# Scaling the probabilities instead of the heads' output in a latent attention, with the query transposes moved ahead

## The reference, cut to what matters

```python
q = (c_q @ w_uq).reshape(b, s_len, MLA_HEADS, MLA_NOPE + MLA_ROPE)
q = jnp.concatenate([q[..., :MLA_NOPE], apply_rope(q[..., MLA_NOPE:], positions)], axis=-1)
...
logits = jnp.einsum('bqhd,bkhd->bhqk', qb, kb).astype(jnp.float32) * scale
logits = jnp.where(causal, logits, NEG_INF)
probs = jax.nn.softmax(logits, axis=-1).astype(v.dtype)
outs.append(jnp.einsum('bhqk,bkhd->bqhd', probs, vb))
...
return o.reshape(b, s_len, MLA_HEADS * MLA_V) @ w_o
```

## Time and profile before

| | us |
|---|---|
| median of three runs (1433.08 to 1433.68) | 1433.24 |
| the profiled execution, its own time | 1433.6 |
| its span, first to last instruction | 1431.8 |
| TensorE busy (8258 matmuls) | 1416.1 |
| TensorE's weight loads busy | 1234.8 |
| VectorE busy | 657.7 |
| ScalarE busy | 747.8 |
| GpSimd busy | 1058.2 |

### The profile page before, as it was taken

How to read it: one execution, slowest core, us unless ns; L and a number is a source line. 1 busy time by engine, 2 the same in 40 slices (tenths; PEclk the granted TensorE clock), 3 DMA queues, 4 the chain that set the end, 5 groups by cost and what they waited for, 6 DMA issues and landing times.

```text
span 1431.8 us, 20732 instructions
## 1 busy us (share of the span) xinstructions
PE 1416.1 (99%) x8258; PEld 1234.8 (86%) x8258; DVE 657.7 (46%) x1379; ACT 747.8 (52%) x985; POOL 1058.2 (74%) x262
## 2 busy tenths in 40 slices
PE   9999999999999999999999999999999999999997
PEld 7888888888899899888888889988888899888886
DVE  5546555034333333355440354656650566556614
ACT  7876555354666566665543545435543346354540
POOL 5475988965766656869888677749889577688891
PEclk9999999999999999999999999999999999999999
DMA  7576555546655656455554565255555655365560
GB/s 252 207 270 221 182 201 181 202 164 201 206 172 189 195 178 197 162 192 192 190 188 165 202 245 195 102 206 177 196 214 200 222 187 180 118 232 180 192 220 29
DMA packets 65239, 272.12 MB, mean 190 GB/s; under 512 B 6186, under 2 KB 28896, under 8 KB 38529
## 3 DMA queue, kind: packets, MB, share of 16 engines
q1 hardware_dynamic: 40280, 243.36, 49.7%
q10 hardware_dynamic: 24873, 27.53, 5.7%
HBM read 269.73 MB, written 8.21 MB: 194 GB/s over the span
## 4 chain that ended last, share of the span: by engine, by line
PE 94%; ACT 2%; DVE 2%; DMA 0%; issue 0%; SPq 0%; POOL 0%; DVEq 0%; ACTq 0%
PE psum L487 90%; PE psum L690 1%; PE psum L997 1%; PE psum L576 1%; PE psum L834 1%; ACT prob L1422 0%; ACT w_hi L1188 0%; PE psum L877 0%; DMA raw<-w_mla_a 0%; DVE xt_both L1762 0%; ACT q_rows L1389 0%; PE psum L1146 0%; PE psum L1103 0%; DVE psum L2142 0%; DVE psum L2129 0%
## 5 line engine op out<-in xcount | busy, mean ns | idle before, releaser
L479 POOL TENSOR_TENSOR w_lo<-raw,w_hi 128x2048 fp32r<-128x2048 f32 (+2 forms) x248 | 1044.8, 4230 | 336.9 <-ACT w_hi L1188 336.5
L1188 ACT ACTIVATE w_hi<-raw 128x2048 fp32r<-128x2048 f32 (+2 forms) x248 | 432.6, 1754 | 134.8 <-DMA raw<-w_tail 85.9
L487 PE MATMUL psum<-xt_both,w_hi 128*128 128x512 f32 (+1 forms) x1888 | 434.8, 370 | 0.0
L487 PEld LDWEIGHTS psum<-xt_both,w_hi 128*128 128x128 f32 x1888 | 334.8, 189 | 55.8 <-issue 3.6
L487 PE MATMUL psum<-w_hi,xt_both 128*128 128x512 f32 (+3 forms) x1104 | 309.2, 365 | 0.3 <-ACT w_hi L1323 0.2
L487 PE MATMUL psum<-xt_both,w_lo 128*128 128x256 f32 x1696 | 249.4, 283 | 0.0
L487 PEld LDWEIGHTS psum<-xt_both,w_lo 128*128 128x128 f32 x1696 | 229.6, 191 | 7.4
L487 PEld LDWEIGHTS psum<-w_hi,xt_both 128*128 128x128 f32 x1104 | 200.6, 188 | 26.8 <-issue 1.1
L487 PE MATMUL psum<-w_lo,xt_both 128*128 128x512 f32 (+3 forms) x552 | 191.0, 362 | 0.2
L1278 ACT ACTIVATE lanes<-lanes 128x256 f32<-128x256 f32 x88 | 36.8, 418 | 156.2 <-DVE lanes L1799 108.0
L487 PEld LDWEIGHTS psum<-w_lo,xt_both 128*128 128x128 f32 x552 | 102.6, 188 | 13.1 <-POOL w_lo L474 1.1
(11 more groups left out here) (225 smaller groups left out, 1401.6 us busy)
## 6 DMA issues: line engine op xcount, KB each, us to landing
raw<-w_tail SPq DMA_DIRECT2D x156, 1024.0 KB, 4.8
raw<-w_dil SPq DMA_DIRECT2D x24, 1024.0 KB, 4.8
raw<-w_mix SPq DMA_DIRECT2D x24, 1024.0 KB, 4.9
raw<-w_dil SPq DMA_DIRECT2D x16, 576.0 KB, 3.8
bias_tiles<-bias_rows ACTq DMA_DIRECT2D x1, 6912.0 KB
gbuf<-gain_rows ACTq DMA_DIRECT2D x12, 512.0 KB, 5.5
dbias<-bias_tiles ACTq DMA_DIRECT2D x16, 384.0 KB, 6.1
raw<-w_dil SPq DMA_DIRECT2D x8, 384.0 KB, 4.5
```

Of the source, the lines that this page charges most:

```text
L479: nc.gpsimd.tensor_tensor(w_lo[:, s, 0:width], raw[:, s, 0:width], w_hi[:, s, 0:width].bitcast(F32), ALU.subtract).then_inc(lo_split, 1)
L487: return nc.tensor.matmul(dst, lhsT, rhs, start=start, stop=stop)
L1188: nc.scalar.activation(w_hi[:, s, 0:width], raw[:, s, 0:width], ACT.Copy).then_inc(hi_split, 1)
```

## The change

Each head's probabilities are multiplied by the inverse of their row sum on VectorE, in `prob0`, before TensorE transposes them. The near sums are inverted together and four products over 128 columns follow, ahead of the rotation of the query rows (`mla_scale_near`). Behind the rotation, each far head is awaited by itself, inverted and multiplied over 256 columns (`mla_scale_far`). ScalarE signals each far exponential by itself. The spread on TensorE, the copy to `over0` and the product on bank 7 are gone, and `ot_hi` waits for the value products directly. On TensorE the query rows are transposed ahead of the probabilities and the key rows behind them; the transposes of the near probabilities wait for the near products, those of the far for the far products. In the last step all of `wo1(0)` stands ahead of the probabilities, and `mla_sum` stands in the middle of `wo2(0)`.

```diff
-            def mla_turn(step):
+            def mla_turn_q(step):
 
                 pe.wait_ge(roped, step + 1)
                 turn_heads(q_rows, 3).then_inc(q_turned, 1)
+
+            def mla_turn_k(step):
+
                 pe.wait_ge(heads_copied, step + 1)
                 turn_heads(k_rows, 5).then_inc(k_turned, 1)
...
-                if not first:
-                    pe.wait_ge(over_ready, step)
...
             def mla_probs(step):
-                pe.wait_ge(exped, 2 * step + 2)
-                for j in range(3 * MLA_GROUP):
-                    ins = nc.tensor.transpose(flat[:, j * P:(j + 1) * P], prob0[:, j * P:(j + 1) * P], ident[:, :])
+                for qb, part in enumerate((range(MLA_GROUP), range(MLA_GROUP, 3 * MLA_GROUP))):
+                    pe.wait_ge(p_scaled, 2 * step + qb + 1)
+                    for j in part:
+                        ins = nc.tensor.transpose(flat[:, j * P:(j + 1) * P], prob0[:, j * P:(j + 1) * P], ident[:, :])
                 ins.then_inc(p_turned, 1)
...
                 pe.wait_ge(pt_ready, step + 1)
-                pe.wait_ge(sums_inverted, step + 1)
-                for j in range(MLA_GROUP // 2):
-                    for qb in range(2):
-                        ins = spread(0, j * SEQ + qb * P, qb, 2 * j)
-                ins.then_inc(sums_spread, 1)
...
                 mla_scores(step)
                 mla_gemm(step + 1)
+                mla_turn_q(step + 1)
                 mla_probs(step)
-                mla_turn(step + 1)
+                mla_turn_k(step + 1)
                 mla_sum(step, lambda: pe.wait_ge(ot_ready, step))
...
             wo1 = wo_part(0, 1)
-            wo1(0, lambda: mla_probs(last))
-            mla_sum(last, lambda: None)
+            wo1(0)
+            mla_probs(last)
             pe.wait_ge(ot_ready, 3)
             wo2 = wo_part(0, 2)
-            wo2(0)
+            wo2(0, lambda: mla_sum(last, lambda: None))
...
-                ins.then_inc(exped, 1)
+                    if qb == 1:
+                        ins.then_inc(exped, 1)
+                if qb == 0:
+                    ins.then_inc(exped, 1)
...
             def mla_out(step):
-                act.wait_ge(o_scaled, step + 1)
+                act.wait_ge(o_summed, step + 1)
...
-            def mla_invert(at):
-                dve.wait_ge(exped, 2 * at + 2)
-                v.reciprocal(rinv_q[:, :, :], rsum_q[:, :, :]).then_inc(sums_inverted, 1)
+            def mla_scale_near(at):
+                dve.wait_ge(exped, (1 + MLA_GROUP) * at + 1)
+                step(v.reciprocal(rinv_q[:, 0, :], rsum_q[:, 0, :]))
+                for hh in range(MLA_GROUP):
+                    part = prob0[:, hh * P:(hh + 1) * P]
+                    ins = v.tensor_scalar(part, part, rinv_q[:, 0, hh:hh + 1], None, ALU.mult)
+                ins.then_inc(p_scaled, 1)
+
+            def mla_scale_far(at):
+                for hh in range(MLA_GROUP):
+                    dve.wait_ge(exped, (1 + MLA_GROUP) * at + hh + 2)
+                    step(v.reciprocal(rinv_q[:, 1, hh:hh + 1], rsum_q[:, 1, hh:hh + 1]))
+                    part = prob0[:, MLA_GROUP * P + hh * SEQ:MLA_GROUP * P + (hh + 1) * SEQ]
+                    ins = v.tensor_scalar(part, part, rinv_q[:, 1, hh:hh + 1], None, ALU.mult)
+                ins.then_inc(p_scaled, 1)
 
             def mla_out(at):
-                dve.wait_ge(sums_spread, at + 1)
-                v.tensor_copy(over0[:, :], psum[:, 0, :]).then_inc(over_ready, 1)
-                dve.wait_ge(over_ready, at + 1)
-                dve.wait_ge(o_summed, at + 1)
-                v.tensor_tensor(psum[:, 7, :], psum[:, 7, :], over0[:, :], ALU.mult).then_inc(o_scaled, 1)
                 dve.wait_ge(o_hi, at + 1)
...
                 mla_softmax(at)
+                mla_scale_near(at)
                 mla_rope(at + 1)
-                mla_invert(at)
+                mla_scale_far(at)
                 mla_kT(at + 1)
                 mla_out(at)
...
             mla_softmax(MLA_STEPS - 1)
-            mla_invert(MLA_STEPS - 1)
+            mla_scale_near(MLA_STEPS - 1)
+            mla_scale_far(MLA_STEPS - 1)
             mla_out(MLA_STEPS - 1)
```

More of the change, by code:

```diff
@@ L229, in build @@
             probT0 = sb("probT0", [P, MLA_GROUP * 3, P], F32, part)
-            over0 = sb("over0", [P, BANK], F32, part)
             table = sb("table", [BUCKETS + 1, heads_all], F32, part)
@@ L348, in build @@
         exped = sem("exped")
[L349 to L352, removed]
+        p_scaled = sem("p_scaled")
         p_turned = sem("p_turned")
@@ L844, in mla_turn_first, with mla_scores @@
                 pe.wait_ge(heads_copied, 1)
-            def mla_turn(step):
+            def mla_turn_q(step):
                 pe.wait_ge(roped, step + 1)
                 turn_heads(q_rows, 3).then_inc(q_turned, 1)
+            def mla_turn_k(step):
                 pe.wait_ge(heads_copied, step + 1)
                 turn_heads(k_rows, 5).then_inc(k_turned, 1)
-            def mla_scores(step, first=False):
-                if not first:
-                    pe.wait_ge(over_ready, step)
+            def mla_scores(step):
                 pe.wait_ge(q_ready, step + 1)
@@ L904, in _ @@
                 bias(g)
-            mla_scores(0, True)
+            mla_scores(0)
             mla_gemm(1)
+            mla_turn_q(1)
             mla_probs(0)
-            mla_turn(1)
+            mla_turn_k(1)
             mla_sum(0, lambda: pe.wait_ge(brow_out, NG + 1))
@@ L1986, in _ @@
             mla_step(0)
-            with loop(MLA_STEPS - 2, 3) as i:
+            with loop(MLA_STEPS - 2, 8) as i:
                 mla_step(i + 1)
             mla_softmax(MLA_STEPS - 1)
-            mla_invert(MLA_STEPS - 1)
+            mla_scale_near(MLA_STEPS - 1)
+            mla_scale_far(MLA_STEPS - 1)
             mla_out(MLA_STEPS - 1)
```

## The result

| | before | after |
|---|---|---|
| median, us | 1433.28 (1433.08 to 1433.68, 4 runs) | 1445.99 (1444.26 to 1446.66, 4 runs) |
| profiled execution: time / span | 1433.6 / 1431.8 | 1445.71 / 1443.9 |
| granted TensorE clock | 0.999 | 0.994 |
| TensorE busy (matmuls) | 1416.1 (8258) | 1417.2 (8194) |

The change makes the kernel slower by 12.7 us; the ratio is 1.0087, 95% interval 1.0069 to 1.0104. The forecast was +10.3, 1443.5, in a range of 1436.5 to 1447.

The account below looks back on a forecast made before the run. TensorE was taken as the bound, busy for 1416 of 1431.8 us. Steps 0 to 3 at +2.4, -0.1, +1.2 and +6.8 sum to 10.3, on the median 1433.24 giving 1443.5, range 1436.5 to 1447.

Parts of the forecast that it names:

- step 0: First latent-attention step: near products and query rotation wait behind two GpSimd splits; 2.4 us longer.
- step 1: Second latent-attention step, where GpSimd's split ends early enough: 14.91 us long, a change of -0.1.
- step 2: Third latent-attention step: GpSimd's 2048-column split holds the first near product, delaying the rotation; 1.2 us longer.
- step 3: Last latent-attention step: two near products wait for queued splits, then ot_hi stands behind w_hi copies; wo3 6.8 us later.
- GpSimd's hold: VectorE's new SBUF products in the attention wait out GpSimd's splits, one product between two; sum +10.3, forecast chance 0.64.
- Rival 1: The attention's new products are not held by GpSimd: sum +2.9 (+4.5), 1436.1 to 1437.7; chance 0.14.
- Rival 2: The products are held once, then VectorE keeps its turn between instructions: sum 5.9, 1439.1; chance 0.12.
- S: Start of a step's score matmuls; places in a step are given as S plus a number of us.
- The free step: Latent-attention step without other trouble, step 1: 14.91 us, a far head taking 0.465 and its product 0.35.
- The moved cover: Query transposes moved ahead no longer cover ScalarE's probability copy: TensorE waits about 0.75 us per step before the value products.
- the two w_hi parts: ScalarE's copies standing in front of ot_hi in the last step: a TensorE wait of some 1.7 us before wo3.
- Rival 4: Products run at 0.483, or a further split falls in far products of step 0 or 2: +2 to +5; chance 0.05.

Follow-up runs that it names:

- e9: Changed kernel with filler matmuls in TensorE's waits, 9 in step 0 and 18 in step 3: 1443.29 us, ratio 1.0072.
- e1: Changed kernel with the near inverses in PSUM and one 512-column near product, far products unchanged: 1441.74 us, ratio 1.0058.
- e10: e7 with the products of the change (tensor_scalar, inverse in SBUF, four near products for one): 1442.20 us, ratio 1.0061.
- e7: e4 with the far exponentials ahead of ScalarE's copy of the query rows: 1429.93 us, ratio 0.9976.
- e2: Changed kernel with the query transposes put back behind the transposes of the probabilities: 1447.81 us, ratio 1.0097.
- e5: Changed kernel with near and far inverses in PSUM for every product, order of engines unchanged: 1437.55 us, ratio 1.0028.
- e3: Changed kernel with the last step's ot_hi put ahead of ScalarE's two w_hi copies: 1446.07 us, ratio 1.0089.
- e6: Changed kernel with filler matmuls in TensorE's waits, 18 in step 0 and 36 in step 3: 1446.56 us, ratio 1.0090.
- e8: Kernel before the change with only the far exponentials moved ahead of the copy of the query rows: 1433.52 us, ratio 1.0000.
- e4: Changed kernel with all inverses in PSUM, far products before the rotation, TensorE's earlier order and ot_hi before w_hi: 1432.88 us, ratio 0.9996.

## Why the prediction was right

The forecast was of the right sign and mechanism and 2.5 too low (1445.99 against 1443.5). The profiled executions are 12.1 apart, and the terms are compared there:

| term | forecast | after | without the fallen clock (e9) |
|---|---|---|---|
| step 0 | +2.4 | +3.24 | +2.11 |
| step 1 | -0.1 | -0.10 | -0.10 |
| step 2 | +1.2 | +1.02 | +1.02 |
| step 3 | +6.8 | +7.26 | +6.40 |
| outside the attention | 0 | +0.7 | -0.2 |
| sum | +10.3 | +12.1 (spans) | +9.2 |

**GpSimd's hold** was the step on which all hung, with one two-element cast as evidence. It is shown: the same four products take 0.88 free and 4.16, 2.87 and 9.04 beside splits; in the other form one product does their work in 0.69 beside splits (e1); and with nothing but the form changed the time moves by 12.3 (e10 against e7). Rival 1 is out. Rival 2 (held once, not between instructions) is out by step 3 of after, where two near products in a row take 4.18 and 4.55 and end at S+10.27 and S+14.74 (10.15 and 14.9 forecast), and by e1, where two far products in a row are held by two splits in a row.

**The free step**: 14.91 forecast, 14.86 measured; the far head has a pitch of 0.46 (0.465 forecast), its product takes 0.35 as estimated from the copy's row.

**The moved cover**: a wait of 0.75 before the value products forecast, 0.67 measured three times. Against the spread of 0.93 it is no loss, and e2 shows that putting it back wins nothing while VectorE is late.

**Step 3**: the near transposes were to start near S+15.5 and started at S+15.2; the wait in front of them was to be 4 to 5 and was 4.12. Before wo3 I expected 1.7 for the two w_hi parts: 1.00 in after, 1.42 in e9 and e5. The term is right in kind, its size a little high. The forecast did not ask what is late next if ot_hi goes first: the norm's squares (e3).

**What the forecast lacked.** The clock term is missing from it altogether. It named waits of 4 us and priced the work behind them at full clock; e9 puts the clock at 2.0 of the 12.1. The 0.7 outside goes with the one long DMA issue; 0.56 of it is seen as a wait. With both, the sum would have been 10.3 + 2.0 + 0.7 = 13.0; the terms of the held steps were 0.9 too high together. In steps 0, 2 and 3 the far transposes began 0.2 to 0.3 earlier than forecast (in e9 at S+12.90, 11.62 and 17.05; forecast 13.13, 11.79 and 17.36), and 1.42 and not 1.7 stood before wo3. So that the forecast lies as near as it does is in part luck: what it lacked and what it had too high have opposite signs. Rival 4 (a further split in the far products) did not occur in after; e1 ran into its like in step 3. The range was said to take in rivals 1 and 2, but at 1436.5 it starts above the 1436.1 of rival 1.

Left open: why single DMA issues of ScalarE's queue take 2 us and more. One of 1.9 to 2.8 is in the profiles of after, e1 to e5, e7 and e10; before, e6, e8 and e9 have none. Every profile, that of before too, has one of 1.4 to 1.9 some 300 us behind step 0. No experiment was made on it.

## What to carry to other kernels

Before giving VectorE a product within SBUF, look at what GpSimd has queued at that time: with splits waiting back to back, each such product may cost a whole split, whatever its own size (4.55 for 128 columns, 4.42 for 256), so the price is set by the number of instructions and not by their width. The form with the inverse in PSUM is slower by itself (0.42 against 0.35) and was free of this in every run; but taking one instruction out of the hold passes it to the next of the old form, so look at all of them: changing the near ones gave 4.3 of the 12.7 back, changing all gave 8.4. And when a forecast holds idle stretches on TensorE like the two here (2.16 and 4.12), price the work behind them at the lower clock as well; it came to 1.1 and 0.9.

## What the runs showed of the hardware that was not expected

- **The clock behind a wait.** Around waits of 2.16 and 4.12 the granted clock was 0.50 for 3.4 and some 6.8 us, and eight or twelve transposes took up to twice their time (1.97 against 1.09 for eight). Behind the shorter wait it did not fall in every execution: e3 had 2.14 there and kept the clock, with a step 1.13 shorter. Nor does it take one long wait: in step 0 of e10 it fell behind waits of 0.82 and 1.19 with four transposes between them. The runs of after spread over 2.4 us, against 0.6 before and 0.95 in e9 with the clock kept. That the clock makes this spread isn't shown: after's runs at 1444.26 and 1446.27 have mean clocks of 0.995 and 0.996.
- **The alternation of VectorE and GpSimd.** Between two queued splits of 4.6 us VectorE got one tensor_scalar product, as after's 4.18 and 4.55 and e1's 3.46 and 4.42 show; reciprocals (0.15 to 0.17) and products with an input in PSUM ran through.
- **A DMA issue of 2.2 us.** The issue from ScalarE's queue that takes 0.51 as a rule took 2.21 in after, 2.4 to 2.8 in e1, e2, e3 and e4, 2.18 in e5 and e7 and 1.94 in e10; the time was lost on TensorE only in part (a wait of 0.56 in after, 0.30 in e10, 1.14 in e2).
